# The last attention pair's transposes in front of the output rows, and two fillers moved

## The chip, the cores and the metric

The kernel runs on 1 core of one Trainium2 chip. The metric is the device time of one execution in microseconds. The engines are TensorE (PE, with its weight loads as PEld), VectorE (DVE), ScalarE (ACT), GpSimd (POOL) and SyncE (SP, here the queue that issues the weight loads).

## The reference, cut to what matters

Three transformer layers over one sequence of 256 tokens of width 1024, in fp32. Layer 0 has the attention of this case:

```python
def mixer_ab(h, w_in, w_out, cmp_wk, cmp_wv, cmp_pe, sinks, rel_table):
    proj = h @ w_in
    ...
    o_a = nsa_attention(qa.reshape(B, S, H, dh), ...)      # 8 heads: compressed + selected + window, gated
    o_b = swa_sink_attention(qb.reshape(B, S, H, dh), ...) # 8 heads, sliding window with a sink
    return jnp.concatenate([o_a, o_b], axis=-1) @ w_out

def first_block(...):
    for layer in range(DEPTH):
        ...
        h = rms_norm(x, norm_w[layer, 0, 0]) * (1.0 + scale) + shift
        y = mixer_ab(...) if layer % 2 == 0 else mixer_cd(...)
        x = x + gate * rms_norm(y, norm_w[layer, 0, 1])
        ...
        h = rms_norm(x, norm_w[layer, 1, 0]) * (1.0 + scale) + shift
        x = x + gate * rms_norm(swiglu(h, ...), norm_w[layer, 1, 1])
```

The second block adds two more feed-forward networks with a mixer (short convolution and a state-space part) between them. Each sublayer begins with the same step: norm the rows of x, scale and shift them.

## The kernel before

**Data.** A weight arrives in 255 chunks of 128 x 2048 fp32 through 5 buffers (`rawt`). Each chunk has two halves. ACT makes the high part of a half (HI, one copy with rounding, in `high`), DVE the low part (LO = raw - HI, in `low`), and TensorE multiplies three times: high by high, low by high, high by low. Activations are split in the same way into HH (ACT) and HLo (DVE). HI and LO have 6 slots; a slot is free when TensorE has used the half in it. `Walk` fixes the order of halves; `catch_up(unit - 1, 1)` converts one half more than is due, `weight` converts up to four ahead.

**Stages.** Layer 0's mixer ("ab", then its output projection "abo"), feed-forward "f0", layer 1 ("cd", "cdo", "f1"), and the second block ("f2", "in2" with "o2", "f3"). Every engine has its own instruction stream, written out by hand; semaphores join them, and an engine does its stream in order. So an instruction that waits holds back all that stands behind it on its engine.

**The attention of layer 0** has 18 units of work (i = 0 to 17) in 9 pairs. For a unit: TensorE makes scores (`scores`), DVE adds the bias and finds the maximum (`biased`), ACT takes the exponential (`exps`), DVE scales by the sum (`scaled`), TensorE transposes four tiles of 128 x 128 (`transposes`), ACT copies the result to SBUF (`moved`), and TensorE multiplies by the values (`values`). Units 0 to 11 add up in PSUM banks 0 and 1, units 12 to 17 in banks 2 and 3. The loop runs over pairs p; in iteration p the transposes are those of pair p - 2 and the values those of pair p - 3, so two pairs of transposes and three of values are left for after the loop.

**The output rows.** `out_parts(name, i)` reads PSUM bank i and writes tiles 2i and 2i + 1 of HH (ACT) and HLo (DVE): the inputs of the output projection. `out_half(name, ks, qt)` multiplies the tiles ks for the row half qt, six matmuls of 512 columns for a tile. Row half 0 goes to PSUM banks 0 and 1, so even tile 0 waits for HLo of tile 3:

```python
w.wait_ge(*A.at(("hh", name, k)))
w.wait_ge(*D.at(("hlo", name, 7 if qt else max(k, 3))))
```

Tile k uses weight half k of "abo". After the rows of both halves come the norm of the result and the sum with x (`add_normed`).

**The start of a sublayer.** In `modulate(tag, sc, fill)` TensorE transposes the rows of x, first half 0, then half 1, each as soon as that half of X is written, and then broadcasts a diagonal that holds the rows' factors (key "rb", input `dg` from DVE, the instruction of L1400). ACT copies the broadcast, and DVE and ACT then make HH and HLo tile by tile. `fill` gives three numbers of matmuls whose result nobody reads (`busy_wide`): in front of the wait for half 0, in front of that for half 1, and in front of the wait for the diagonal.

```python
for qt in range(2):
    busy_wide(fill[qt])
    ...
    w.wait_ge(*D.at(("x", tag, qt)))
    ...
busy_wide(fill[2])
ps = take(("rb", tag))
w.wait_ge(*D.at(("dg", tag)))
```

Lines in the profile: L408 every matmul, L608 the transposes of the attention, L540 those of x, L940 every ACT instruction, L1351 the low weight half, L1433 HLo of the output tiles, L1532 to L1540 `scaled`, L1555 `biased`.

Of the kernel before, what the change touches and what calls it, by code (L numbers as in the profile page):

```python
# [189 lines left out]
def build(nc, xT, small, vecs, ssm, consts, firsts, WS, scratch, gates_out, out):  # L190
# [15 lines left out]
    with ctx:  # L206
# [67 lines left out]
        def turned(k):  # L274

            return PS[:, k % 4, k // 4 * 256:k // 4 * 256 + 256]
# [124 lines left out]
        def pe(e):  # L401
            w = Waits(e)
            walk = Walk(plan, units, where, order)
# [16 lines left out]
            def busy_wide(n):  # L420
                idle[0] += 1
                key = ("idle", idle[0])
                ps = take(key)
                for i in range(n):
                    mm(ps[:, :], HH[:, 0, 0:128], flat(HH[:, 0:2, :]), True, True)
                banks.give(key)
# [10 lines left out]
            def mods(col):  # L437
                walk.mods(col)
# [87 lines left out]
            def modulate(tag, sc, fill=(0, 0, 0)):  # L526

                mods(sc + 8)
                for qt in range(2):
                    busy_wide(fill[qt])  # L530
                    if tag == "ab":
                        w.wait_ge(*XIN.at("in"))
                        w.wait_ge(*CONST.at("in"))
                    else:
                        w.wait_ge(*D.at(("x", tag, qt)))
                        w.wait_ge(*D.at(("gy", tag, 3)))
                        if tag not in ("in2", "f3"):
                            w.wait_ge(*A.at(("sq", tag, 2)))
                    for k in range(8):
                        e.transpose(turned(k)[:, qt * 128:qt * 128 + 128], X[:, qt, k * 128:k * 128 + 128], C("ident"))  # L540
# [3 lines that stand above are left out]
                mm(ps[:, 0:256], nones[:, :], RS[:, 2, :], True, True).then_inc(*P.up(("rb", tag)))  # L544
                banks.give(("rb", tag))
# [71 lines left out]
            def values(tag, U_, p):  # L617

                pair = (2 * p, 2 * p + 1)
                for i in pair:  # L620
                    w.wait_ge(*A.at(("free", ("t", tag, i))))
                nh, nk = U_[2 * p][9], U_[2 * p][8] + 1
                steps = [(n, kt) for n in range(0, nh, 2) for kt in range(nk)]
                for n, kt in steps:
                    for i in pair:
                        vcol, b, last, qt, h0 = [U_[i][x] for x in (2, 4, 7, 8, 10)]
                        g, pr = h0 // 4, (h0 + n) % 4
                        p4 = p_slot(tag, i).rearrange("p (h k n) -> p k h n", h=nh, k=nk)
                        x = pv(b, pr, g, o_ap(b, pr, g, qt), VT[:, kt, vcol + g * 64:vcol + g * 64 + 64],
                               p4[:, kt, n:n + 2, :], last and kt == nk - 1)  # L630
                        if (n, kt) == steps[-1]:
                            x.then_inc(*P.up(("v", tag, i)))

            def out_half(name, ks, qt):

                for k in ks:
                    key = (name, k // 2)
                    wt = weight(key, k % 2)
                    w.wait_ge(*A.at(("hh", name, k)))
                    w.wait_ge(*D.at(("hlo", name, 7 if qt else max(k, 3))))  # L640
                    rows(name, (HH, HLo), k, wt, k == 0, k == 7, [used(key, k % 2)] if qt else [], (qt,))
# [109 lines left out]
            for p in range(9):  # L751
                scores("ab", AB, p)
                if p > 1:
                    transposes("ab", p - 2)
                walk.spare(2)
                for f in compressed.get(p, ()):
                    f()
                if p > 5:
                    walk.catch_up(walk.unit - 1, 1)
                if p > 2:  # L760
                    values("ab", AB, p - 3)
            transposes("ab", 7)
            values("ab", AB, 6)
            out_half("abo", (0, 1), 0)
            transposes("ab", 8)
            values("ab", AB, 7)
            out_half("abo", (2, 3), 0)
            values("ab", AB, 8)
            out_half("abo", (4, 5), 0)
            out_half("abo", (0, 1), 1)  # L770
            out_half("abo", (6, 7), 0)
# [88 lines left out]
            ffn("f1", turn, 88)  # L860
            modulate("f2", 104, (8, 4, 4))
            ffn("f2", lags, 112)
            modulate("in2", 128, (0, 8, 4))

            def drive():

# [62 lines left out]
            banks.give(("xs", "ssmy"))  # L929
            out_half("o2", range(4, 8), 0)  # L930
            out_half("o2", range(4, 8), 1)
            modulate("f3", 152, (0, 8, 4))
            ffn("f3", lambda j: None, 160)

        def act(e):
            w = Waits(e)
            walk = Walk(plan, units, where, order)
# [59 lines left out]
            def out_parts(tag, i):  # L997
                parts(tag, 2 * i, PS[:, i, :].rearrange("p (a b) -> p a b", a=2))
# [75 lines left out]
            def moved(tag, i):  # L1074
                w.wait_ge(*P.at(("t", tag, i)))
                if i > 3:
                    w.wait_ge(*P.at(("v", tag, i - 4)))
                fn(p_slot(tag, i), bank(("t", tag, i)), F.Copy).then_inc(*A.up(("free", ("t", tag, i))))
# [79 lines left out]
            for p in range(9):  # L1158
                for i in (2 * p, 2 * p + 1):
                    if p > 1:  # L1160
                        moved("ab", i - 4)
                for i in (2 * p, 2 * p + 1):
                    exps("ab", i, *AB[i])
                high(walk.spare(2))
                for f in compressed.get(p, ()):
                    f()
                if p > 5:
                    high(walk.catch_up(walk.unit - 1, 1))
            w.wait_ge(*P.at(("v", "ab", 11)))
            out_parts("abo", 0)  # L1170
            moved("ab", 14)
            moved("ab", 15)
            out_parts("abo", 1)
            moved("ab", 16)
            moved("ab", 17)
            use(("abo", 0), 0)
# [152 lines left out]
        def dve(e):  # L1329
            w = Waits(e)  # L1330
            walk = Walk(plan, units, where, order)
# [12 lines left out]
            def low(us):  # L1344
                for j, h in us:
                    if plan[j][0] == "mod":
                        gemv(j, plan[j][1], h)
                    elif plan[j][0] == "w":
                        s = order[j, h]
                        w.wait_ge(*A.at(("hi", s)))  # L1350
                        e.tensor_tensor(LO[:, s % HL, :], raw_half(j, h), HI[:, s % HL, :].bitcast(fp32),  # L1351
                                        O.subtract).then_inc(*D.up(("lo", s)))

            def use(key, half, ahead=AHEAD):
                low(walk.weight(key, half, ahead))
                walk.done(key, half)
# [46 lines left out]
            def modulate(tag, sh):  # L1403
                if tag != "ab":
                    next_weights(tag, 4)
                    roots(tag)
                w.wait_ge(*D.now())

                def rest(k):
                    w.wait_ge(*A.at(("hh", tag, k)))  # L1410
                    e.scalar_tensor_tensor(HLo[:, k, :], TMP[:, k, :], MV[:, sh + k:sh + k + 1],  # L1411
                                           HH[:, k, :].bitcast(fp32), O.add, O.subtract).then_inc(*D.up(("hlo", tag, k)))

                for k in range(8):
                    w.wait_ge(*A.at(("free", ("rb", tag))))
                    e.scalar_tensor_tensor(TMP[:, k, :], turned(k), AV[:, k:k + 1], RS[:, 3, :], O.mult, O.mult) \  # L1416
                        .then_inc(*D.up(("tmp", tag, k)))
                    if tag == "ab" and k == 1:
                        low(walk.catch_up(walk.unit - 1, 1))
                    if k:  # L1420
                        rest(k - 1)
                rest(7)
# [13 lines left out]
            def out_parts(tag, i):  # L1436
                parts(tag, 2 * i, PS[:, i, :].rearrange("p (a b) -> p a b", a=2))
# [196 lines left out]
            for p in range(9):  # L1634
                for i in (2 * p, 2 * p + 1):
                    biased("ab", i, *AB[i])
                for i in (2 * p - 2, 2 * p - 1):
                    if p > 0:
                        scaled("ab", i, *AB[i])
                low(walk.spare(2))  # L1640
                for f in compressed.get(p, ()):
                    f()
                if p > 5:
                    low(walk.catch_up(walk.unit - 1, 1))
            scaled("ab", 16, *AB[16])
            scaled("ab", 17, *AB[17])
            out_parts("abo", 0)
            out_parts("abo", 1)
            use(("abo", 0), 0)
            use(("abo", 0), 1)  # L1650
            out_parts("abo", 2)
# [397 lines left out]
        @block.tensor  # L2049
        def _(e):  # L2050
            pe(e)
# [163 lines left out]
```

## Time and profile before

| | |
|---|---|
| median of 3 runs | 1276.33 us (1276.31 to 1277.69) |
| profiled execution | 1275.76 us, span 1274.0 us |
| mean granted TensorE clock | 0.959 |
| busy share PE / PEld / DVE / ACT / POOL | 92% / 83% / 73% / 46% / 6% |
| chain that ended last | PE 69%, DVE 19%, ACT 5%, DMA 5% |

Times in the rows are microseconds from the start of the span. The profiled execution's own time is 1.76 us above its span. A line of the timeline gives start, duration, engine, line, operation, count and in brackets the idle time of the engine before it with what ended it. Instructions of one engine overlap in the pipeline, so the next one can start before a duration is over.

### The profile page before, as it was taken

The numbers are of one execution on the slowest core, as the hardware profiler recorded it, in microseconds if no ns is written. First come the engines' busy times: TensorE is split into PE (matmuls) and PEld (weight loads), VectorE is DVE, ScalarE is ACT, GpSimd is POOL, SyncE is SP. The second block draws the span as 40 slices with busy tenths as digits, with TensorE's granted clock in tenths as the row PEclk, the third lists the DMA queues.
The fourth block names the chain that finished last, engine by engine and source line by source line (L and its number), as shares of the span: only waits on it lengthen the run. The fifth ranks groups of instructions, "written<-read, shape, count | busy, mean of one in ns | idle before, by whom it ended". The sixth has DMA issues, their size and how long they took to land.

```text
span 1274.0 us, 19995 instructions
## 1 busy us (share of the span) xinstructions
PE 1168.5 (92%) x8366; PEld 1057.0 (83%) x8366; DVE 933.2 (73%) x1630; ACT 589.5 (46%) x968; POOL 74.4 (6%) x106
## 2 busy tenths in 40 slices
PE   2798789999998987999999989999989998999997
PEld 1687468899897975789999979999979977999996
DVE  5967848888786955589987688887765957765445
ACT  1534645344345445553544464454443365444443
POOL 0000000000000000069100000000000000000000
PEclk8899889999999998999999999999999998999999
DMA  9982324788893860257789637779742452665830
GB/s 375 360 355 81 162 106 156 307 308 320 279 336 129 347 240 9 102 213 281 292 212 388 248 130 279 292 290 279 277 155 96 109 160 101 240 234 203 200 133 33
DMA packets 40810, 280.83 MB, mean 220 GB/s; under 512 B 4736, under 2 KB 5264, under 8 KB 7952
## 3 DMA queue, kind: packets, MB, share of 16 engines
q1 hardware_dynamic: 37296, 269.27, 58.4%
q0 software_dynamic: 2416, 7.92, 2.1%
q10 hardware_dynamic: 1008, 2.37, 0.5%
q8 instruction: 65, 1.06, 0.3%
q14 instruction: 25, 0.20, 0.1%
HBM read 277.91 MB, written 1.10 MB: 219 GB/s over the span
## 4 chain that ended last, share of the span: by engine, by line
PE 69%; DVE 19%; ACT 5%; DMA 5%; issue 1%; SPq 0%; DVEq 0%; ACTq 0%
PE PS L408 69%; DVE LO L1351 5%; DMA raw<-WS 4%; DVE raw L1341 4%; ACT HI L940 2%; DMA SC<-scratch 1%; DVE TMP L1416 1%; DVE HLo L1411 1%; DVE TMP L1451 1%; DVE SC L1555 1%; ACT SC L940 1%; ACT HH L940 1%; ACT SQ L940 1%; DVE SC L1540 1%; DVE RS L1555 1%
## 5 line engine op out<-in xcount | busy, mean ns | idle before, releaser
L408 PE MATMUL PS<-HH,HI 128*128 128x256 f32 x1748 | 502.3, 287 | 26.1 <-ACT HH L940 22.3
L408 PE MATMUL PS<-HLo,HI 128*128 128x256 f32 x1748 | 503.1, 288 | 0.7 <-DVE HLo L1411 0.2
L408 PE MATMUL PS<-HH,LO 128*128 128x256 f32 x1748 | 499.5, 286 | 0.0
L1351 DVE TENSOR_TENSOR LO<-raw,HI 128x1024 fp32r<-128x1024 f32 x340 | 403.9, 1226 | 122.6 <-ACT HI L940 122.4
L940 ACT ACTIVATE HI<-raw 128x1024 fp32r<-128x1024 f32 x340 | 339.9, 1048 | 90.8 <-PE PS L408 60.2
L408 PEld LDWEIGHTS PS<-HH,HI 128*128 128x128 f32 x1748 | 340.5, 195 | 35.2 <-DVE LO L1351 19.3
L408 PEld LDWEIGHTS PS<-HH,LO 128*128 128x128 f32 x1748 | 340.2, 195 | 3.3 <-issue 0.5
L408 PEld LDWEIGHTS PS<-HLo,HI 128*128 128x128 f32 x1748 | 339.7, 194 | 3.7 <-DVE HLo L1411 2.7
L1341 DVE CUSTOM_DVE_ANT_0 raw<-raw,CB,SM 128x1024 f32<-128x1024 f32 x168 | 210.5, 1285 | 22.3 <-DMA raw<-WS 22.2
L408 PE MATMUL PS<-HI,HDH 128*128 128x512 f32 x352 | 140.2, 398 | 0.0
L408 PE MATMUL PS<-HI,HDL 128*128 128x512 f32 x352 | 139.5, 396 | 0.0
L408 PE MATMUL PS<-LO,HDH 128*128 128x512 f32 x352 | 138.9, 395 | 0.0
L940 ACT ACTIVATE HDH<-FB 128x256 fp32r<-128x256 f32 x88 | 36.8, 418 | 208.4 <-DVE FB L1512 208.4
L940 ACT ACTIVATE FB<-PS 128x256 f32<-128x256 f32 (+1 forms) x94 | 37.9, 404 | 130.6 <-PE PS L408 130.5
L940 ACT ACTIVATE SC<-PS 128x512 f32<-128x512 f32 (+3 forms) x65 | 36.1, 572 | 95.7 <-PE PS L408 67.7
L408 PEld LDWEIGHTS PS<-HI,HDL 128*128 128x128 f32 x352 | 66.4, 189 | 15.9
L408 PEld LDWEIGHTS PS<-LO,HDH 128*128 128x128 f32 x352 | 66.5, 189 | 12.8
L408 PEld LDWEIGHTS PS<-HI,HDH 128*128 128x128 f32 x352 | 66.4, 189 | 12.4
L408 PE MATMUL PS<-HI,HH 128*128 128x512 f32 (+2 forms) x176 | 63.4, 361 | 12.7 <-DVE HLo L1433 8.0
L1512 DVE TENSOR_TENSOR FB<-FB,PS 128x256 f32<-128x256 f32 x88 | 36.7, 417 | 52.2 <-ACT FB L940 52.1
L1515 DVE TENSOR_TENSOR HDL<-FB,HDH 128x256 fp32r<-128x256 f32 x88 | 37.7, 428 | 45.9 <-ACT HDH L940 45.9
L408 PE MATMUL PS<-LO,HH 128*128 128x512 f32 (+2 forms) x176 | 62.7, 356 | 0.0
(230 smaller groups left out, 1038.0 us busy)
## 6 DMA issues: line engine op xcount, KB each, us to landing
raw<-WS SPq DMA_DIRECT2D x255, 1024.0 KB, 5.9
SC<-scratch POOLq DMA_DIRECT2D x2, 1024.0 KB, 13.3
FB<-gates_out POOLq DMA_DIRECT2D x3, 512.0 KB, 4.7
SQ<-gates_out POOLq DMA_DIRECT2D x3, 512.0 KB, 9.6
X<-xT ACTq DMA_DIRECT2D x1, 1024.0 KB, 6.8
SC<-ssm POOLq DMA_DIRECT2D x2, 512.0 KB, 4.4
out<-TMP SPq DMA_DIRECT2D x2, 512.0 KB, 2.6
CB<-vecs SPq DMA_DIRECT2D x1, 512.0 KB, 6.4
```

Of the source, the lines that this page charges most:

```text
L408: return e.matmul(o, l, r, start=start, stop=stop, skip_group_check=True)
L940: return e.activation(o, a, f, **k)
L1341: e.tensor_tensor_reduce(x, x, CB[:, :], 1.0, S("mb")[:, c:c + 1], O.mult, O.add, MV[:, c:c + 1]) \
L1351: e.tensor_tensor(LO[:, s % HL, :], raw_half(j, h), HI[:, s % HL, :].bitcast(fp32), O.subtract).then_inc(*D.up(("lo", s)))
L1411: e.scalar_tensor_tensor(HLo[:, k, :], TMP[:, k, :], MV[:, sh + k:sh + k + 1], HH[:, k, :].bitcast(fp32), O.add, O.subtract).then_inc(*D.u ...
L1416: e.scalar_tensor_tensor(TMP[:, k, :], turned(k), AV[:, k:k + 1], RS[:, 3, :], O.mult, O.mult) \
L1451: e.tensor_tensor(gy[qt][:, c], PS[:, b, :], grow(tag)[:, c], O.mult).then_inc(*D.up(("gy", tag, b)))
L1512: e.tensor_tensor(HF[:, j % 2, :], SIL[:, j % 2, :], bank((key, 0))[:, 256:512], O.mult) \
L1515: e.tensor_tensor(HDL[:, j % 3, :], HF[:, j % 2, :], HDH[:, j % 3, :].bitcast(fp32), O.subtract) \
L1540: e.tensor_scalar(s3[:, n, :], s3[:, n, :], gg[:, n:n + 1], None, O.mult) \
L1555: e.tensor_tensor_reduce(s3[:, n, :], bank(("s", tag, i))[:, n * kw:(n + 1) * kw], BI[:, bh + h0 + n, bo:bo + kw], 1.0, sk[:, n:n + 1] if ...
```

## The change

In TensorE's stream the transposes of the last pair, and the values of pair 7, move in front of the first output tile, and the last values in front of tiles 1, 2 and 3. In ACT's stream the two `out_parts` for tiles 0 to 3 stand together in front of the copies of transposes 14 and 15, and the weight half that was converted in the loop's last iteration comes behind these copies. In DVE's stream that half comes behind the scaling of units 16 and 17 and the HLo of tiles 0 to 3. In front of "in2" and "f3" the fillers change from 0, 8 and 4 to 4, 0 and 4.

```diff
@@ TensorE
-                if p > 5:
+                if 5 < p < 8:
                     walk.catch_up(walk.unit - 1, 1)
                 if p > 2:
                     values("ab", AB, p - 3)
             transposes("ab", 7)
             values("ab", AB, 6)
-            out_half("abo", (0, 1), 0)
             transposes("ab", 8)
             values("ab", AB, 7)
-            out_half("abo", (2, 3), 0)
+            out_half("abo", (0,), 0)
             values("ab", AB, 8)
+            out_half("abo", (1, 2, 3), 0)
             out_half("abo", (4, 5), 0)
             out_half("abo", (0, 1), 1)
             out_half("abo", (6, 7), 0)
@@ TensorE
-            modulate("in2", 128, (0, 8, 4))
+            modulate("in2", 128, (4, 0, 4))
@@ TensorE
-            modulate("f3", 152, (0, 8, 4))
+            modulate("f3", 152, (4, 0, 4))
@@ ACT
-                if p > 5:
+                if 5 < p < 8:
                     high(walk.catch_up(walk.unit - 1, 1))
             w.wait_ge(*P.at(("v", "ab", 11)))
             out_parts("abo", 0)
+            out_parts("abo", 1)
             moved("ab", 14)
             moved("ab", 15)
-            out_parts("abo", 1)
+            high(walk.catch_up(walk.unit - 1, 1))
             moved("ab", 16)
             moved("ab", 17)
             use(("abo", 0), 0)
@@ DVE
-                if p > 5:
+                if 5 < p < 8:
                     low(walk.catch_up(walk.unit - 1, 1))
             scaled("ab", 16, *AB[16])
             scaled("ab", 17, *AB[17])
             out_parts("abo", 0)
             out_parts("abo", 1)
+            low(walk.catch_up(walk.unit - 1, 1))
             use(("abo", 0), 0)
```

## Rows read from the trace of the kernel before

**Rows 1.** The page: busy times, and the chain that ended last by engine.

```profile
PE 1168.5 (92%) x8366; PEld 1057.0 (83%) x8366; DVE 933.2 (73%) x1630; ACT 589.5 (46%) x968; POOL 74.4 (6%) x106
...
PE 69%; DVE 19%; ACT 5%; DMA 5%; issue 1%; SPq 0%; DVEq 0%; ACTq 0%
```

**Rows 2.** The chain in order of time: start, us, what.

```profile
183.86 10.53 PE PS L408 x45
...
210.42 1.19 DVE raw L1341
```

**Rows 3.** Timeline of PE, end of the attention: start, us, what, idle before.

```profile
160.82 1.98 PE L408 MATMUL PS<-SC 128*64 128x256 f32 x8
164.62 0.77 PE L408 MATMUL PS<-HI,HH 128*128 128x512 f32 x1 [1.83 <-DVE HLo L1433]
...
170.54 0.60 PE L608 MATMUL PS<-CN,SC 128*128 128x128 f32 x4
171.07 1.08 PE L408 MATMUL PS<-SC 128*64 128x256 f32 x8
172.08 0.50 PE L408 MATMUL PS<-HI,HH 128*128 128x512 f32 x1
...
174.09 0.50 PE L408 MATMUL PS<-HI,HH 128*128 128x512 f32 x1 [0.34 <-DVE LO L1351]
...
177.05 0.47 PE L408 MATMUL PS<-HI,HH 128*128 128x512 f32 x1 [0.31 <-DVE HLo L1433]
```

**Rows 4.** Timeline of DVE, the same stretch.

```profile
160.21 1.23 DVE L1351 TENSOR_TENSOR LO<-raw,HI 128x1024 fp32r<-128x1024 f32 x1 [0.36 <-ACT HI L940]
161.36 0.15 DVE L1532 TENSOR_TENSOR SC<-SC 128x2 f32<-128x2 f32 x1
...
163.20 1.28 DVE L1433 TENSOR_TENSOR HLo<-PS,HH 128x512 fp32r<-128x512 f32 x2
```

**Rows 5.** Timeline of ACT, the same stretch.

```profile
159.14 1.04 ACT L940 ACTIVATE HI<-raw 128x1024 fp32r<-128x1024 f32 x1
...
160.56 1.06 ACT L940 ACTIVATE SC<-PS 128x512 f32<-128x512 f32 x2
...
171.71 2.95 ACT L940 ACTIVATE HI<-raw 128x1024 fp32r<-128x1024 f32 x3
```

**Rows 6.** Stretches of 1 us: length, busy PE, PEld, DVE, ACT, POOL, granted clock, DMA share, GB/s.

```profile
160.00:161.00 1.00, 1.00 (x6) 0.67 (x8) 0.79 (x1) 1.00 (x3) 0.00 (x0) 0.54 0.00 0
...
170.00:171.00 1.00, 1.00 (x9) 0.90 (x7) 0.00 (x0) 0.26 (x1) 0.00 (x0) 0.84 0.00 0
```

**Rows 7.** Timelines of PE, DVE and ACT at the start of in2.

```profile
944.14 2.10 PE L408 MATMUL PS<-HH 128*128 128x512 f32 x8
946.07 1.03 PE L540 MATMUL PS<-CN,X 128*128 128x128 f32 x8
...
943.20 1.23 DVE L1483 TENSOR_TENSOR X<-X,TMP 128x1024 f32<-128x1024 f32 x1
...
946.86 0.48 DVE L1400 TENSOR_SCALAR RS<-CN,NR 128x128 f32<-128x128 f32 x2
...
948.50 0.38 ACT L940 ACTIVATE RS<-PS 128x256 f32<-128x256 f32 x1 [2.27 <-PE PS L408]
```

**Rows 8.** Timelines of DVE and ACT at the start of f3.

```profile
1071.06 0.48 DVE L1400 TENSOR_SCALAR RS<-CN,NR 128x128 f32<-128x128 f32 x2
...
1072.69 0.38 ACT L940 ACTIVATE RS<-PS 128x256 f32<-128x256 f32 x1 [2.26 <-PE PS L408]
```

**Rows 9.** The chain in order of time at the start of f0.

```profile
201.70 0.49 DVE RS L1400 x2
...
202.98 0.39 ACT RS L940
```

**Rows 10.** Stretches of 1 us in f3, columns as in rows 6.

```profile
1074.00:1075.00 1.00, 0.72 (x3) 0.51 (x4) 0.82 (x3) 0.62 (x2) 0.00 (x0) 0.93 0.89 377
...
1078.00:1079.00 1.00, 1.00 (x9) 1.00 (x9) 1.00 (x4) 0.55 (x2) 0.00 (x0) 0.87 0.00 0
```

## The prediction

> **What bounds the kernel now.** I read the page first. TensorE is busy 92% of the span and carries 69% of the chain that ended last, DVE 19% [rows 1]. So a microsecond is won where that chain stands still on TensorE or is waiting for DVE, not where an engine is merely busy. Then I read the chain in the stretch of the edit. After the attention of layer 0 come 45 matmuls of 512 columns in 10.53 us, which is 0.234 us each or 1.40 us for one output row half (six matmuls), and from 210 us on DVE's weight work carries the chain of the first feed-forward stage [rows 2]. Both follow whatever ends before them; nothing there is tied to a clock time.
>
> The timeline of TensorE shows what the edit is about. The values of pair 6 end at 160.82 + 1.98 = 162.80. Then TensorE idles 1.83 us, until 164.62, for the low parts of output tiles 0 to 3. Only behind the 12 matmuls of tiles 0 and 1 come the transposes of the last pair, its predecessor's values, tiles 2 and 3 with a wait of 0.34 us for a low weight half, the last values, and at 177.05 tile 4, with 0.31 us waited for HLo [rows 3]. DVE shows why the 1.83 us exist: it converts a weight half first (160.21, start to next instruction 1.15 us), then scales units 16 and 17 (161.36 to 163.20), and only then writes HLo [rows 4]. ACT finishes the last exponentials at about 159.14, makes the high weight half, the first HH, and copies transposes 14 and 15 from 160.56 [rows 5]. The granted clock is at half (1.2 GHz) from about 160.1 (0.54 in that microsecond) to 170.3 (0.84) [rows 6]: inside that stretch TensorE pauses at 162.80.
>
> **The edit around the last pair.** DVE now scales 16 and 17 straight after 14 and 15, so the 1.15 us of the low half leave the front: scaled at 163.20 - 1.15 - 0.36 (it no longer waits for the high half) = 161.7 [rows 4]. ACT writes both HH at 159.2 to 160.3 and copies 14 and 15 to about 161.5; the high half follows, by 162.5 [rows 5]. HLo of tiles 0 to 3 takes DVE 1.28 us more, to 163.0. All of this is earlier than TensorE asks for it: at 162.80 the last transposes find their input, the values of pair 7 find their copies, tile 0 comes later still. The 1.83 us are gone.
>
> Next, what is left between 162.80 and tile 4, at the full clock: eight transposes 2 x 0.53 = 1.06 (170.54 to 171.07), values of pair 7 1.01 (171.07 to 172.08), tiles 0 to 3 4 x 1.40 = 5.60, last values 1.0; together 8.67 us [rows 2, 3]. At half clock each takes twice as long (the values 1.98 against 1.01). If the clock rises at R, tile 4 starts at R + 8.67 - (R - 162.8)/2 = R/2 + 90.07. The same count for before, whose slow work starts at 164.62 and which has 0.65 us of waits, gives 170.3 + 8.67 - (170.3 - 164.62)/2 + 0.65 = 176.8 against the 177.05 of the trace.
>
> Are the two later waits also gone? The low half for tile 3 came late because ACT reached it at 171.71, after copies 16 and 17, which stood behind tiles 0 and 1 on TensorE [rows 3, 5]. Now those copies are possible at about 164 and 165, so the three high halves (2.95 us) run to 168 and the low ones to about 169.3; tile 3 asks at 171 or later. HLo of tiles 4 to 7 is then written by 171, before tile 4. What is moved back, the third weight half, is converted by 164.2 and first used by tile 2, after 168. Its cover is some 4 us; it would cost its 1.15 us only if that were gone. The DMA issues behind it on SP wait for low halves that now come earlier. Banks are taken in the same order as before. The wait for the first unit freed by row half 1 stays and moves with the rest.
>
> What is unknown is R. In the feed-forward stage of f3 the clock fell at 1074.86 and rose at 1078.26, after 3.4 us of matmuls without a pause [rows 10]. Before, here, the matmuls restarted at 164.62 and the rise came at 170.3, 5.7 us later [rows 3, 6]. After the edit the transposes end at about 162.80 + 2.1 = 164.9, and from there matmuls run without a break. So R is 164.9 + 3.4 = 168.3 by the nearer row and 164.9 + 5.7 = 170.6 by the later one; if the transposes are no break, matmuls run from 160.82 and R = 164.2. I take 168.3: TensorE has no pause after it, as in f3. Tile 4 starts at 174.22 instead of 177.05: **2.83 us** won. The bounds are 1.68 us (R = 170.6) and 4.88 us (R = 164.2).
>
> Whether transposes count matters here. The rows show no rise while transposes and values 6 ran up to 162.80, with the pause behind them; the rise came after 12 matmuls in a row. The Trainium skill (TensorE: Matmul & The Clock Gate, Part 4: PE-mode transpose) says that a transpose does not count as TensorE being busy in the way a matmul does. By it, drawing eight of them into the slow stretch speaks against the early rise and for 1.7 to 2.8 us; without it 4.9 us are open. No row here tests it alone.
>
> **The fillers in front of in2 and f3.** The filler of eight matmuls stood between the two halves' transposes. In in2 the second half of X is written by 943.20 + 1.23 = 944.4, but the filler (944.14, 2.10 us) holds its transposes back to 946.1 [rows 7]. Now four fillers run before the first half arrives, in idle time, and none between. Transposes then end at about 945.4 and the last four fillers (about 0.9 us) at 946.3. The row broadcast is now held by the diagonal that DVE starts at 946.86. In the f0 stage, where the broadcast waits for exactly that, ACT's copy started 202.98 - 201.70 = 1.28 us after DVE's start [rows 9]. So 946.86 + 1.28 = 948.14 against 948.50: 0.36 us [rows 7]. In f3, 1071.06 + 1.28 = 1072.34 against 1072.69: 0.35 us [rows 8]. Together **0.71 us**. The cost that they could bring is a clock that falls sooner, since four matmuls fewer run. It already falls at 1074.86 in f3 [rows 10]. Nothing below 0 is excluded; one more slow stretch of 3.4 us does 1.7 us less work, so each place lies between +0.36 and -1.35 us.
>
> **The sum.** 2.83 + 0.71 = 3.54 us. The profiled execution took 1275.76 us (span 1274.0); less 3.54 is 1272.2. The median of before is 1276.33, 0.57 us above it; with that I predict **1272.8 us**. About 0.2%, 2.55 us, is what a measurement of this kernel can tell from no change, so the line is 1273.8.
>
> **The rivals.**
>
> (a) Forecast: the pause and both waits gone, R between 167 and 169.5. Time 1272.2 to 1273.4. Chance 0.42.
>
> (b) The clock rises early, R near 164.2, because TensorE is busy from 160.82 on. 4.88 + 0.71 = 5.59 us, 1270.7 us. For it: no idle gap at 162.80 any more. Against it: the busy stretch up to 162.80 brought no rise in before. Chance 0.22.
>
> (c) The clock rises as late as before or still later, because transposes are no work in the eyes of the clock gate. 1.68 + 0.71 = 2.39 us, 1273.9; with R = 173.7 only 0.8 us, 1275.5. For it: the matmuls of 512 columns now start at about 167 instead of 164.62. Chance 0.22; its time straddles the line. It is the way that the page TensorE: Matmul & The Clock Gate of the Trainium skill (Part 4: PE-mode transpose) would have it.
>
> (d) The gain is given back later, since the first feed-forward stage waits for DVE and weights, or since the new fillers cost a slow stretch each (2 x 1.7 us): in the second case the 0.71 us turn into -2.7: 1276.33 - 2.83 + 2.7 = 1276.2, in the first it is 1276.3 less 0.71 at most. Against the first: DVE's work there starts from the modulated rows, and weight buffers are freed by DVE's own low halves, so both move. Chance 0.10.
>
> (e) Slower: the clock stays at half through tiles 0 to 3, since the dense matmuls are now cut into one tile, values, three tiles. From R = 173.96 on this part loses, and from 175.4 the whole. At R = 180.5 it is 2.55 us slower, 1278.9. Against it: values count as matmuls and leave no gap, and even before a gap of 1.83 us the slow stretch was 10.2 us. Chance 0.04.
>
> **How the numbers follow.** Faster by over 0.2%: nearly all of (a) and (b), 0.62, and a third of (c), 0.07: 0.69. Within: the rest of (c), (d): 0.27. Slower: 0.04. The range goes from below (b), 1270.4, to (c) with a late rise, 1275.2; what is left out is most of (d), (e) and the tail of (c), under 0.2. The likeliest case's own range is 1272.2 to 1273.4.
>
> **What the profile of the changed kernel would show.** Right: TensorE's transposes of the last pair start within 0.2 us of the end of the values before them, no wait above 0.2 us before tile 4, which starts near 174.2; scaled units 16 and 17 before the LO instruction on DVE; the granted clock back at 1.0 near 168; ACT's copy of the broadcast about 0.4 us sooner after the write of X in in2 and f3. Wrong: a wait of TensorE for HH, for copies 14 and 15 or for LO at tiles 2 and 3; a slow stretch that reaches beyond 171; a second slow stretch in in2 or f3.

## The result, and the profile after

The changed kernel takes 1269.07 us (median of 4 executions, 1267.86 to 1270.36) against 1276.32 (1275.31 to 1277.69); the ratio is 0.9945 with an interval of 0.993 to 0.9959. It is faster, 7.25 us by the medians, where 3.5 were forecast, and 1.3 us under the predicted range. The profiled execution took 1268.52 us, span 1266.7.

TensorE's timeline at the end of the attention (start, us, instruction, idle before), which answers to [rows 3]:

```profile
161.09 1.98 PE L408 MATMUL PS<-SC 128*64 128x256 f32 x8
163.00 1.12 PE L608 MATMUL PS<-CN,RS 128*128 128x128 f32 x4
163.91 0.66 PE L608 MATMUL PS<-CN,SC 128*128 128x128 f32 x4
164.50 1.08 PE L408 MATMUL PS<-SC 128*64 128x256 f32 x8
165.51 0.50 PE L408 MATMUL PS<-HI,HH 128*128 128x512 f32 x1
...
167.10 1.08 PE L408 MATMUL PS<-SC 128*64 128x256 f32 x8
168.12 0.50 PE L408 MATMUL PS<-HI,HH 128*128 128x512 f32 x1
...
172.34 0.39 PE L408 MATMUL PS<-HI,HH 128*128 128x512 f32 x1
```

None of these instructions has idle time before it: the pause of 1.83 us and the waits of 0.34 and 0.31 us of [rows 3] are gone. Tile 4 starts at 172.34, where it stood at 177.05. The stretches of 1 us show the granted clock: it is the seventh figure, behind the length and the busy times of PE, PEld, DVE, ACT and POOL, and 0.50 is half clock:

```profile
160.00:161.00 1.00, 0.80 (x5) 0.47 (x4) 0.93 (x5) 1.00 (x3) 0.00 (x0) 0.81 0.12 49
...
163.00:164.00 1.00, 1.00 (x7) 1.00 (x6) 1.00 (x2) 0.00 (x0) 0.00 (x0) 0.50 0.00 0
164.00:165.00 1.00, 1.00 (x11) 0.69 (x11) 0.41 (x1) 0.85 (x2) 0.00 (x0) 0.99 0.00 0
```

It falls to 1.2 GHz at about 160.6 and is back at 2.4 GHz at 164.0. That is a slow stretch (time at half clock) of 3.4 us; in [rows 6] it lasted from 160.1 to 170.3, 10.2 us. DVE, whose order is shown here, does what the prediction said:

```profile
161.47 0.62 DVE L1541 TENSOR_SCALAR SC<-SC 128x256 f32<-128x256 f32 x2
162.00 1.28 DVE L1434 TENSOR_TENSOR HLo<-PS,HH 128x512 fp32r<-128x512 f32 x2
163.20 1.22 DVE L1352 TENSOR_TENSOR LO<-raw,HI 128x1024 fp32r<-128x1024 f32 x1
166.21 3.50 DVE L1352 TENSOR_TENSOR LO<-raw,HI 128x1024 fp32r<-128x1024 f32 x3 [1.80 <-ACT HI L940]
```

Unit 17 is scaled by 162.0, HLo of tiles 0 to 3 follows, the moved half comes last (163.20), and the three low halves behind it begin at 166.21 and are done before tile 3 asks, after 170.

Where the 7.24 us between the two profiles lie can be read from DVE's writes of X, which close each stage (start times in us, before and after; where a stage ends with both row halves of X, it is the second write):

| stage, up to | before | after | won in the stage |
|---|---|---|---|
| transposes of unit 14 begin | 159.07 | 159.47 | -0.40 |
| second write of X, layer 0 | 197.82 | 193.03 | 5.19 |
| end of f0 | 402.32 | 397.74 | -0.21 |
| end of layer 1's attention | 538.05 | 531.78 | 1.69 |
| end of f1 and f2 | 943.20 | 936.89 | 0.04 |
| first write in front of f3 | 1062.01 | 1055.03 | 0.67 |
| last write | 1265.17 | 1257.93 | 0.26 |

### The profile page after: what moved, and what is told of

It reads as the page before. It is cut to its first block, busy times and chain, and to the rows that moved or that the text cites. A ratio compares the mean times of both kernels' runs of the same rounds, so it can differ in the third digit from the quotient of the medians.

```text
span 1266.7 us, 19978 instructions
## 1 busy us (share of the span) xinstructions
PE 1159.9 (92%) x8358; PEld 1049.2 (83%) x8358; DVE 933.0 (74%) x1630; ACT 589.4 (47%) x968; POOL 74.4 (6%) x106
## 4 chain that ended last, share of the span: by engine, by line
PE 69%; DVE 19%; ACT 6%; DMA 5%; issue 1%; SPq 0%; DVEq 0%; ACTq 0%
PE PS L408 68%; DVE LO L1352 5%; DMA raw<-WS 4%; DVE raw L1342 4%; ACT HI L940 2%; DMA SC<-scratch 1%; DVE TMP L1417 1%; DVE SC L1556 1%; DVE TMP L1452 1%; DVE HLo L1412 1%; ACT HH L940 1%; ACT SQ L940 1%; ACT SC L940 1%; DVE SC L1541 1%; DVE RS L1556 1%
## 5 line engine op out<-in xcount | busy, mean ns | idle before, releaser
L408 PE MATMUL PS<-HI,HH 128*128 128x512 f32 (+2 forms) x176 | 62.3, 354 | 10.2 <-DVE HLo L1434 5.8
```

The lines of the kernel that those rows point to most:

```text
L408: return e.matmul(o, l, r, start=start, stop=stop, skip_group_check=True)
```

## The experiments

Three distances are used as yardsticks. A: from the start of the transposes of unit 14 to the second write of X in layer 0 (before 38.75, after 33.56). B: from the second write of X in front of in2 to the first in front of f3 (118.81 and 118.14). For f3: from the second write in front of it to the last write (197.76 and 197.46).

**The attention edit alone** (`e1_attention`): the changed kernel with the fillers put back.

```diff
-            modulate("in2", 128, (4, 0, 4))
+            modulate("in2", 128, (0, 8, 4))
-            modulate("f3", 152, (4, 0, 4))
+            modulate("f3", 152, (0, 8, 4))
```

> The edit around the last attention pair alone, fillers as before. Clock theory (no pause before the output tiles, and transposes count as work, so the clock is back about 3.4 us after it fell): 5.2 us of the 7.25 come from here, time about 1271.0, the clock rises near 164. Waits theory (only the pause of 1.83 us and the two waits of 0.65 us are won, the rest is a chance of the profile): 2.5 us, about 1273.8. Fillers theory (in2 and f3 give more than 0.9 us): this one gains under 4 us and the next one the rest.

Measured: median 1269.53 us of 12 executions against 1275.03 of 35, ratio 0.9962 (0.9947 to 0.9977). A is 33.47. The means differ by 4.6 us (1269.98 against 1274.61). The waits theory is out: its 2.5 us lie below the 2.9 us at which the interval begins. The profile also showed something not expected, in front of in2 (the chain in order of time):

```profile
933.41 1.64 PE PS L540 x8
935.05 2.87 PE PS L408 x8
937.93 0.87 PE PS L540 x8
```

The 8 fillers stand on the chain, and here they take 2.87 us instead of 1.85, and the transposes before them 1.64 instead of 1.07, since the clock was at half from 933.8 to 937.2.

**The fillers alone** (`e2_fillers`): the kernel before with the two filler lines of the change.

```diff
-            modulate("in2", 128, (0, 8, 4))
+            modulate("in2", 128, (4, 0, 4))
-            modulate("f3", 152, (0, 8, 4))
+            modulate("f3", 152, (4, 0, 4))
```

> The two filler edits alone. Clock and waits theories: 0.7 to 0.9 us, time about 1275.5, within what can be told from no change; slow stretch in in2 3.4 or 6.8 us as the chance falls. Fillers theory: 2 us or more, at or under 1274.3, with a shorter slow stretch in in2 and f3.

Measured: 1271.92 us, ratio 0.9973 (0.9958 to 0.9987), 3.4 us by the means of the set. B is 117.20, f3 197.40. So alone, on the old order, the fillers give more than forecast. But the profiled execution, with 1267.71 us the fastest of the twelve, also had a short slow stretch at the output tiles with the old order: A is 36.12, not 38.75. The clock rose at 162.6, after TensorE had gone idle at about 162.1:

```profile
162.00:163.00 1.00, 0.15 (x2) 0.00 (x0) 1.00 (x3) 0.00 (x0) 0.00 (x0) 0.71 0.00 0
```

The length of that stretch differs between executions, and with it part of every difference. The 35 executions of the kernel before in this set range from 1270.62 to 1278.01 us.

**Work in the pause** (`e3_gap_matmuls`, and with transposes `e4_gap_transposes`): the kernel before, nothing reordered.

```diff
             values("ab", AB, 6)
+            busy(4)          # e3: 8 matmuls of 256 bf16 columns; e4 has turn_idle(8): 8 transposes of the identity
             out_half("abo", (0, 1), 0)
```

> The kernel before with 8 matmuls of 256 bf16 columns on zeros in the pause before output tile 0; nothing reordered. Clock theory: TensorE has no pause, the clock is back by about 165 instead of 170.3, the 12 matmuls of tiles 0 and 1 take some 2.8 us instead of 5.3, and 2 to 2.6 us are won although the pause stays: 1274. Waits theory: no gain, 1276.3.

> As the kernel with matmuls in the pause, but with 8 transposes of the identity instead. If transposes count as work for the clock: the same as there, a rise by about 165 and 1274. If they do not: the clock rises near 170 as before and the time is 1276.3.

Measured: 1272.61 us, ratio 0.9992 (0.9977 to 1.0006), and 1271.64 us, 0.9989 (0.9977 to 1.0001). A is 36.11 and 36.10. The clock was back at about 163.0 and 162.8, under 0.7 us into the added work and before tile 0, as it was in `e2_fillers` without anything in the pause. So these profiles don't tell whether the work in the pause did it, and the ratios with their intervals don't exclude that nothing changed, though the medians lie 2.4 and 3.4 us under the 1275.03 of the same set. The single times lean the same way: above 1274 us were 3 of 12 and none of 12, and 24 of the 35 of the kernel before. But `e2_fillers`, with nothing in the pause, has none of 12 there either, so these counts prove nothing about the pause.

**Which engine's order counts** (`e5_half_first`, `e6_pe_order`, `e7_act_dve_order`), old fillers. The first has TensorE's new order and the third weight half in its old place on ACT and DVE, the second has TensorE's new order alone, the third ACT's and DVE's alone:

```diff
# e6, on the kernel before, TensorE only
             values("ab", AB, 6)
-            out_half("abo", (0, 1), 0)
             transposes("ab", 8)
             values("ab", AB, 7)
-            out_half("abo", (2, 3), 0)
+            out_half("abo", (0,), 0)
             values("ab", AB, 8)
+            out_half("abo", (1, 2, 3), 0)
# e7, on the kernel before: the loop's catch-ups, alike on ACT (high) and DVE (low) and in TensorE's count of halves
-                if p > 5:
+                if 5 < p < 8:
# e7, ACT; DVE has low(walk.catch_up(walk.unit - 1, 1)) added behind its out_parts("abo", 1)
             out_parts("abo", 0)
+            out_parts("abo", 1)
             moved("ab", 14)
             moved("ab", 15)
-            out_parts("abo", 1)
+            high(walk.catch_up(walk.unit - 1, 1))
             moved("ab", 16)
# e5, on the changed kernel with the old fillers, at high(...) and low(...); the late catch-ups are taken out again
-                if 5 < p < 8:
+                if p > 5:
```

> The attention edit with TensorE's new order, but the third weight half left in the loop's last iteration on ACT and DVE, in front of the scaling of units 16 and 17; old fillers. Measured from the start of the transposes of unit 14 to the first write of X, the new order takes 25.3 us and the old one 28.0 or 30.6 us with an early or late rise of the clock. Order theory: the transposes of the last pair wait some 0.4 us, 25.8 us, and the clock still comes back after 3.4 us. If 'last pair scaled first' carried the gain: 26.5 us or more.

> TensorE's new order alone, ACT, DVE and fillers as before. Order theory: as with the half first, 25.8 us between the same two events and some 4 us faster than before in the median. If ACT's and DVE's order were needed: a new wait of over 1 us at output tile 0 for HLo, 26.5 us or more.

> ACT's and DVE's new order alone, TensorE's and the fillers as before. Order theory: the pause falls from 1.83 to about 0.5 us, the wait at tile 3 stays, 26.7 us between the same two events with an early rise of the clock, 1 to 3 us faster than before. If TensorE's order carried everything: no gain.

The distances that these three expectations give are A without the stretch to the second write (they count to the first one): 25.3, 28.0 and 30.6 there are 33.5, 36.1 and 38.8 here. Measured: ratios 0.9965 (0.9953 to 0.9978), 0.9961 (0.995 to 0.9973) and 0.9981 (0.9968 to 0.9994); A is 33.70, 33.56 and 36.48. TensorE's order alone gives as much time as the whole attention edit did in `e1_attention` (0.9962). Its timeline in `e6_pe_order`:

```profile
161.96 1.98 PE L408 MATMUL PS<-SC 128*64 128x256 f32 x8
163.87 1.00 PE L608 MATMUL PS<-CN,RS 128*128 128x128 f32 x4
164.71 0.60 PE L608 MATMUL PS<-CN,SC 128*128 128x128 f32 x4
165.24 1.08 PE L408 MATMUL PS<-SC 128*64 128x256 f32 x8
...
167.84 1.08 PE L408 MATMUL PS<-SC 128*64 128x256 f32 x8
```

The transposes find their input without a wait even with DVE's old order, so not even the expected 0.4 us is paid here: at half clock values 6 (1.98 us) take TensorE as long as DVE needs. The profile of `g3_pe_order_fillers` below shows what happens when they run at the full clock. With ACT's and DVE's order alone the pause shrinks and the wait at tile 3 stays, as expected; here the slow stretch lasted 6.8 us:

```profile
162.75 0.77 PE L408 MATMUL PS<-HI,HH 128*128 128x512 f32 x1 [0.55 <-DVE HLo L1434]
...
171.51 0.50 PE L408 MATMUL PS<-HI,HH 128*128 128x512 f32 x1 [0.35 <-DVE LO L1352]
```

**The changed kernel again** (`e8_after_again`).

> The changed kernel again, for more executions. Theory of three sums: order of the attention 2.6 us, a late rise of the clock that the old order meets in two of three executions (1.8 us on average), fillers about 2.3 us: together 6.7, with no execution that has a slow stretch of over 3.4 us at the output tiles. If the result was a lucky profile: the mean gain is 3.5 us or less.

Measured: 1269.94 us (10 executions, 1265.8 to 1273.52), ratio 0.9961 (0.9946 to 0.9976). A is 34.19, B 117.97. The 14 executions of the changed kernel in this set and the first result have a mean of 1269.3, the 88 of the kernel before in all four sets one of 1274.9: 5.6 us, under the first result's 7.25 and under the 6.7 expected. The expectation was also wrong in one point: a slow stretch of 6.8 us does occur. TensorE's timeline there:

```profile
162.06 1.08 PE L608 MATMUL PS<-CN,SC 128*128 128x128 f32 x4 [3.10 <-DVE SC L1533]
162.94 1.07 PE L608 MATMUL PS<-CN,RS 128*128 128x128 f32 x4
163.94 1.98 PE L408 MATMUL PS<-SC 128*64 128x256 f32 x8
165.84 1.12 PE L608 MATMUL PS<-CN,RS 128*128 128x128 f32 x4
166.75 1.06 PE L608 MATMUL PS<-CN,SC 128*128 128x128 f32 x4
```

And its stretches of 1 us:

```profile
161.00:162.00 1.00, 0.00 (x0) 0.00 (x0) 0.91 (x6) 0.99 (x5) 0.00 (x0) 0.50 1.02 434
...
166.00:167.00 1.00, 1.00 (x6) 1.00 (x7) 1.00 (x1) 0.00 (x1) 0.00 (x0) 0.50 0.00 0
167.00:168.00 1.00, 1.00 (x6) 0.61 (x6) 0.01 (x1) 0.74 (x2) 0.00 (x0) 0.66 0.00 0
```

TensorE was idle for 3.10 us, the clock fell in that time (at 160.9), and it comes back at about 167.7. From 162.06 until then TensorE worked without a gap: some 3.7 us of transposes and 1.9 of matmuls, and only transposes since 165.84.

**The fillers taken apart, and the simplest version** (`g1_no_front_filler` with 0, 0, 4; `g2_double_filler` with 0, 16, 4; `g3_pe_order_fillers`: TensorE's new order with 4, 0, 4, and ACT and DVE as before).

```diff
# g1 and g2, on the changed kernel, in2 and f3 alike; g3 is the diff of e6 and that of e2
-            modulate("in2", 128, (4, 0, 4))
+            modulate("in2", 128, (0, 0, 4))    # g2: (0, 16, 4)
```

> The changed kernel with fillers 0, 0, 4 in in2 and f3: the four matmuls in front of the first half are left out. If the gain of the filler edit is only that nothing stands between the two halves' transposes, the stretches are those of the changed kernel: in2 (second write of X there to the first of f3's) 117.2 to 118.1 us, f3 197.4 to 197.5, time within 0.2% of the changed kernel's. If the four in front hold the clock, in2 gets longer by a slow stretch, 1 us or more.

> The changed kernel with fillers 0, 16, 4 in in2 and f3: the suspected cost doubled. Path theory: against 0, 8, 4 (in2 118.2 to 120.7, f3 197.8) each place gets 1.85 us longer at the full clock and up to 3.4 at half, so in2 is 120 us or more and f3 199.6, and the time is some 5 to 6 us above the changed kernel's. If the 8 matmuls were hidden: no difference to 0, 8, 4.

> TensorE's new order and the new fillers, ACT and DVE as in the kernel before. Theory: ACT's and DVE's part of the edit is worth 0.2 us at most, so the time is that of the changed kernel, about 1269.5. If it does carry something that one profile hid: 1 us slower or more.

Measured, in this order: ratio 0.9944 (0.9927 to 0.9961) with B 117.39 and f3 197.38; 0.9995 (0.998 to 1.001) with B 121.01 and f3 199.66; 0.995 (0.993 to 0.997), 1268.82 us, with A 33.37 and B 117.30. One of the six executions of `g1_no_front_filler` took 3745.36 us; the ratio leaves it out, and its cause is not known. The four matmuls in front do nothing that can be seen. Sixteen in the middle are a cost: the mean of `g2_double_filler` is 1274.6 us, 5.3 above the changed kernel's and 4.8 above the 1269.8 of the kernels that have the new order and eight there (`e1_attention`, `e5_half_first`, `e6_pe_order`):

```profile
939.48 1.72 PE L540 MATMUL PS<-CN,X 128*128 128x128 f32 x8 [1.88 <-DVE TMP L1452]
940.85 4.98 PE L408 MATMUL PS<-HH 128*128 128x512 f32 x16
945.67 1.03 PE L540 MATMUL PS<-CN,X 128*128 128x128 f32 x8
```

ACT's and DVE's part of the edit gives nothing that can be seen in the times. It is not without effect, though. In the profile of `g3_pe_order_fillers` the clock did not fall near the output tiles, values 6 took 1.08 us instead of 1.98, and the transposes of the last pair waited 1.10 us for DVE's late scaling:

```profile
164.22 0.66 PE L608 MATMUL PS<-CN,RS 128*128 128x128 f32 x4 [0.84 <-DVE RS L1540]
165.14 0.66 PE L608 MATMUL PS<-CN,SC 128*128 128x128 f32 x4 [0.26 <-DVE SC L1540]
```

So TensorE's order alone suffices when the clock is at half there; at the full clock DVE's order counts too, and A is with 33.37 hardly shorter than the 33.56 of `e6_pe_order` with its 3.4 us at half clock.

**The clock in layer 1** (`g4_layer1_clock`): a slow stretch of 10.2 us or more stands there in every profile but this one.

```diff
             def stick_sums(g):
                 l3 = stick_cube[g % 2][2]
+                if g < 2:
+                    busy((12, 4)[g])       # busy(n) runs 2n matmuls of 256 columns: 24 and 8
```

> The changed kernel with matmuls on zeros in two idle stretches of layer 1's attention (24 of 256 columns before the first sums, 8 before the second), where every profile so far has a slow stretch of 10.2 us. Clock theory: that stretch gets shorter by 3.4 us or more, the time falls by 1 to 3 us against the changed kernel, to about 1267.5. If the fillers are in the way of the sums or the clock falls anyway: no gain or up to 1 us slower.

Measured: 1266.93 us, ratio 0.9931 (0.9919 to 0.9943), the lowest of all. Layer 1's attention with its output takes 132.0 us between the writes of X, against 132.8 to 135.2 (mean 133.8) in the four profiles of the changed kernel. In those TensorE waits 5.1 us for DVE in front of the first sums; here 24 matmuls fill 4.1 of it and 1.00 us is left. The changed kernel's first profile, and this one:

```profile
474.81 1.19 PE L408 MATMUL PS<-SC,CN 128*128 128x256 f32 x2 [5.07 <-DVE SC L1746]
...
470.07 4.13 PE L408 MATMUL PS<-zeros 128*128 128x256 bf16 x24
475.20 0.67 PE L408 MATMUL PS<-SC,CN 128*128 128x256 f32 x2 [1.00 <-DVE SC L1748]
```

The stretches of 1 us around the rise:

```profile
471.00:472.00 1.00, 1.00 (x7) 0.69 (x6) 0.96 (x5) 0.97 (x3) 0.00 (x0) 0.50 0.00 0
472.00:473.00 1.00, 1.00 (x7) 0.74 (x6) 0.93 (x6) 0.97 (x3) 0.00 (x0) 0.58 0.03 4
473.00:474.00 1.00, 1.00 (x11) 0.82 (x9) 0.96 (x6) 0.97 (x2) 0.00 (x0) 1.00 0.88 258
```

The slow stretch now ends at 472.8, before the sums begin, where it had run through them. The changed kernel itself was not run in this set; its ratios in two others are 0.9945 and 0.9961, and the interval of the first overlaps this one. So the gain over it, some 2 us with 5 executions, is likely and not settled.

**How often is the long stretch?** (`h1_before`, `h2_before`, `h4_after`, `h5_after`: one profile each.)

> The kernel before, one more profile. Chance theory: its slow stretch at the output tiles is 10.2 or 3.4 us long as the execution falls; with 10.2 the second write of X in layer 0 comes 38.7 us after the start of the transposes of unit 14, with 3.4 it comes after 36.1 us. If the late rise belongs to the old order: always 38.7 us.

> As the run above: 38.7 or 36.1 us by the chance theory, 38.7 us if the late rise belongs to the order.

> The changed kernel, one more profile. Theory: the slow stretch at the output tiles lasts 3.4 us, or 6.8 us when the clock fell before the transposes of unit 14; the same distance is 33.5 to 34.2 us in any case, so the order takes the chance away as well as the wait.

> As the run above: 33.5 to 34.2 us. A distance above 35 us would show that the new order meets the late rise too.

Measured: 1277.14 and 1277.12 us (the kernel before beside them 1277.37), and 1266.57 and 1265.09 us. A is 38.84 and 38.85 with slow stretches of 10.2 us, and 33.57 and 33.56 with 3.4 us. In `h1_before`:

```profile
166.59 0.77 PE L408 MATMUL PS<-HI,HH 128*128 128x512 f32 x1 [2.03 <-DVE HLo L1433]
...
171.85 0.91 PE L608 MATMUL PS<-CN,RS 128*128 128x128 f32 x4
```

Of the four profiles with the old order and an empty pause, three have the long stretch and one (`e2_fillers`) the short one. All eleven with TensorE's new order have A between 32.9 and 34.5, and none of them has a slow stretch of over 6.8 us there.

The point at which the clock falls differs between executions of the same program, and it allows a fairer comparison. Counted from the start of the transposes of unit 14, it fell after 1.01 to 1.20 us in the three profiles with the long stretch (the first before, `h1_before`, `h2_before`), and after 1.01 to 1.28 us in four with the new order (`e6_pe_order`, the first after, `h4_after`, `h5_after`). From about the same point on, then, the old order had 10.2 us at half clock each time and the new one 3.4. Where the old order had the short stretch (`e2_fillers`, `e3_gap_matmuls`, `e4_gap_transposes`) the clock had fallen earlier, after 0.81 to 0.96 us. That this is what made the stretch short there was not tried.

## Why the prediction was wrong

The wrong step is the value taken for R, the time at which the clock rises: 168.3 where it was 164.0, with the case that had it right, (b), given a chance of only 0.22. The mechanism, no pause on TensorE and an earlier rise, was right.

**The order (right).** Pause and waits gone, transposes ready at 163.0, tile 3 and tile 4 not waited for: 1.83 + 0.65 = 2.48 us. Between kernels with the same early rise it is measured as 36.12 - 33.56 = 2.56. The prediction put the vanished pause down to DVE's new order; `e6_pe_order` reaches it by TensorE's order alone, as long as the clock is at half (`g3_pe_order_fillers` waits 1.10 us at the full clock).

**R (wrong).** 168.3 was taken, the trace has 164.0. The formula itself holds: 164.0/2 + 90.07 = 172.07, and with the late start of this execution (161.09 against 160.82, of which half counts) it is 172.2, measured 172.34. So 2.1 us of the error are R alone, and case (b) with its 4.88 us was right in mechanism: TensorE is busy without a gap, and the transposes did not hold up the rise. I had measured R from the end of the transposes. The size of this term also depends on the execution compared with: against the short slow stretch that the old order had in `e2_fillers` only the 2.56 us are won, against the long one 5.2 to 5.3; the attention edit alone gave 4.6 us by the means, where 2.83 were forecast. The rule of the Trainium skill that a transpose does not count as TensorE being busy in the way a matmul does (TensorE: Matmul & The Clock Gate, Part 4: PE-mode transpose) is not borne out for these fp32 transposes: in `e8_after_again` the clock rose at 167.7 in the midst of them, and two thirds of the work since the idle time were transposes; in the first profile after it rose at 164.0, 1.0 us into them. The place of the rise alone proves little, since in `e2_fillers` the clock rose 0.5 us into the pause. No run had transposes alone in that time, so that they count as fully as matmuls isn't shown. The prediction had leaned on it for rival (c), which did not occur.

**The fillers (mechanism right, size wrong).** 0.71 us were forecast, 0.93 lie between the two profiles. ACT's copy of the broadcast, by which the term was worked out, starts 0.37 us sooner after the write of X in in2 (5.30 before, 4.93 now) and 0.36 us sooner in f3, just as forecast:

```profile
941.82 0.38 ACT L940 ACTIVATE RS<-PS 128x256 f32<-128x256 f32 x1 [1.89 <-PE PS L408]
```

Over all profiles B is 119.67 on average in nine with 0, 8, 4 (118.16 to 120.69) and 117.53 in seven with 4, 0, 4 (117.20 to 118.14), f3 197.8 against 197.4: 2.5 us together. The term was read from one profile, in which the clock was high and the fillers took 1.85 us of the chain; in seven of the nine profiles with 0, 8, 4 the clock is at half there, and in `e1_attention` they take 2.87, with slower transposes in front. The fear that fewer fillers would cost clock found no support: 0, 0, 4 is as good.

The times, however, don't confirm the 2.5 us once the order is changed. The 35 executions with the new order and the old fillers (`e1_attention`, `e5_half_first`, `e6_pe_order`) have a mean of 1269.8 us, the 25 with the new order and four or none in front and none in the middle (first result, `e8_after_again`, `g1_no_front_filler`, `g3_pe_order_fillers`) one of 1269.3: 0.5 us, within the noise. Alone, the attention edit gave 4.6 us and the fillers 3.4; both together gave 5.6, not 8.0. Why the parts don't add up no run shows.

**The rest.** 1.69 us of the first profile's difference lie in layer 1, where nothing was changed. The slow stretch there began earlier and ran less far into the sums. The distance from the end of f0 to the end of that attention is 132.8 to 135.2 us in the other profiles of the changed kernel and 134.9 and 135.3 in the two more of the kernel before, so it was luck of the execution. What the start of in2's and layer 1's stretches depends on beyond that was not tried.

**What did carry through.** The first feed-forward stage gave nothing back: 204.50 and 204.71 us, which fits the argument that DVE's weight work moves with its start, and rival (d) fell. Rival (e) had no sign.

**The chances.** The baseline was read as if an execution were repeatable to 0.2%. Three executions gave 1276.31 to 1277.69; 88 give 1270.4 to 1278.0. The range should have been wider for that alone. By the larger samples the gain is 5.6 us (1269.3 against 1274.9), 2 us above the forecast of 3.5 and just inside the 5.9 us at which the stated range ends (1276.33 - 1270.4); that the first result lay outside it is in part luck.

## What to carry to other kernels

When an engine whose clock depends on its activity waits inside a slow stretch, cost the wait twice: its own length, and the work that may run at half speed for longer because of it; here the pause with the two waits was 2.6 us, and the longer slow stretch another 2.6 in the executions that had it. Look for it in one place: TensorE's stream. Later work that is ready may simply be moved in front of the wait, and the other engines' order may then matter little; look at it again at the full clock. Filler matmuls belong in idle time in front of a wait that comes last; between two inputs of which the second is already there they lengthen the chain, by more when the clock is down. Check by the times of many executions, not only by the profile, whether two gains add up.

## What the runs showed of the hardware that was not expected

Transposes of 128 x 128 in fp32 don't stand in the way of a rise of TensorE's clock: it rose at 167.7 us after 5.6 us of work, 3.7 of them transposes and the last 1.8 nothing else (`e8_after_again`). The same program differs by 7.7 us between executions (1270.4 to 1278.0). Two profiles of the changed kernel, `e8_after_again` and `h5_after`, differ by 6.9 us: 3.1 of them lie before the transposes of unit 14 and 2.2 in layer 1's attention. In both places the slow stretches differ in place or length (in the attentions they last 3.4, 6.8, 10.2 and twice 17.1 us over all profiles); that they make up the whole difference isn't shown.
